# Low weight halves on GpSimd: one operation of 1024 columns, or four of 256

## The reference, cut to what matters

```
x = first_block(...)    # in-projection, short convolution + retention, out-projection, 16-expert FFN (top 32 tokens each)
x = second_block(...)   # in-projection, SSM + LRU mixer, projections, gated FFN with a convolution of 3 taps
return third_block(...) # an even layer (linear attention + sliding window), an odd layer (block attention), norm
```

```
def causal_dwconv(x, w, b):   # second block, K = 4 taps (20 tiles of 128 channels) and 3 taps (48 tiles)
    y[t] = b + sum(w[s] * x[t - s] for s in range(K))
```

## Time and profile before

| | |
|---|---|
| median of the runs | 2131.33 us |
| profiled execution | 2139.45 us |
| its span | 2137.7 us |
| PE busy | 1575.8 us (74%) |
| DVE busy | 758.0 us (35%) |
| POOL busy | 614.3 us (29%), 609.0 of it in L1354 |
| ACT busy | 579.0 us (27%) |
| DMA on the chain that ended last | 37% |

### The profile page before, as it was taken

How to read it: one execution, slowest core, us unless ns; L and a number is a source line. 1 busy time by engine, 2 the same in 40 slices (tenths; PEclk the granted TensorE clock), 3 DMA queues, 4 the chain that set the end, 5 groups by cost and what they waited for, 6 DMA issues and landing times.

```text
span 2137.7 us, 25344 instructions
## 1 busy us (share of the span) xinstructions
PE 1575.8 (74%) x10341; PEld 1066.2 (50%) x10341; DVE 758.0 (35%) x989; ACT 579.0 (27%) x973; POOL 614.3 (29%) x252
## 2 busy tenths in 40 slices
PE   4979786566566765666565689687789787889897
PEld 2758641111111211111111279676779777888797
DVE  3325420000000000000000189797839884176343
ACT  4324430000000000000000234645544344445453
POOL 1144300000000000000000058344648465655473
PEclk8989888877878687887878879899889897998898
DMA  9455559999999999999999825223325332433330
GB/s 395 141 200 229 236 236 428 428 429 428 429 429 428 429 429 428 430 428 428 430 428 429 381 99 186 90 80 118 119 79 197 118 124 112 166 140 113 115 119 20
DMA packets 48292, 570.06 MB, mean 267 GB/s; under 512 B 4576, under 2 KB 10720, under 8 KB 11744
## 3 DMA queue, kind: packets, MB, share of 16 engines
q1 hardware_dynamic: 40992, 556.81, 63.4%
q10 hardware_dynamic: 7232, 12.29, 2.1%
HBM read 564.89 MB, written 4.19 MB: 266 GB/s over the span
## 4 chain that ended last, share of the span: by engine, by line
DMA 37%; PE 29%; DVE 25%; ACT 3%; issue 2%; DVEq 1%; another core or an unknown queue 1%; ACTq 0%; POOL 0%; SPq 0%
PE bank L1373 29%; DMA ring<-in_w_down 12%; DMA ring<-in_w_up 12%; DMA ring<-in_w_gate 12%; DVE work L810 4%; DVE work L157 4%; DVE work L806 3%; DVE work L155 1%; ACT work L1689 1%; DMA ring<-in_dense 1%; DVE work L728 1%; DMA ring<-in_w_ada 1%; DVE rstd L1927 1%; DVE work L1931 1%; ACT weights_high_rounded L1689 1%
## 5 line engine op out<-in xcount | busy, mean ns | idle before, releaser
L1354 POOL TENSOR_TENSOR ring_rounded<-ring,weights_high_rounded 128x1024 fp32r<-128x1024 f32 x244 | 609.0, 2508 | 1475.1 <-ACT weights_high_rounded L1689 1474.3
L1373 PE MATMUL bank<-ring,work 128*32 128x512 f32 x3008 | 483.8, 776 | 309.7 <-DMA ring<-in_w_up 125.3
L1689 ACT ACTIVATE work<-bank 128x256 f32<-128x256 f32 (+3 forms) x312 | 137.5, 447 | 1188.5 <-PE bank L1373 833.4
L1373 PEld LDWEIGHTS bank<-ring,work 128*32 128x32 f32 x3008 | 93.1, 126 | 665.5 <-DMA ring<-in_w_up 207.6
L1689 ACT ACTIVATE weights_high_rounded<-ring 128x1024 fp32r<-128x1024 f32 x244 | 256.0, 1053 | 33.1 <-PE bank L1373 22.3
L1373 PE MATMUL bank<-h_high_rounded,weights_high_rounded 128*128 128x256 f32 x1296 | 208.6, 302 | 54.5 <-ACT weights_high_rounded L1689 35.9
L2140 DVE TENSOR_TENSOR work<-work,bank 128x512 f32<-128x512 f32 x16 | 16.5, 1030 | 592.3 <-PE bank L1373 592.3
L1373 PEld LDWEIGHTS bank<-h_high_rounded,weights_high_rounded 128*128 128x128 f32 x1296 | 178.7, 200 | 74.2 <-issue 39.3
L1373 PE MATMUL bank<-h_normed_rounded,weights_high_rounded 128*128 128x256 f32 x1296 | 187.1, 290 | 0.0
L1373 PE MATMUL bank<-h_high_rounded,ring_rounded 128*128 128x256 f32 x1296 | 182.8, 285 | 2.6 <-POOL ring_rounded L1354 2.5
L1373 PE MATMUL bank<-work_rounded,weights_high_rounded 128*128 128x256 f32 x1088 | 162.6, 301 | 29.1 <-ACT work_rounded L1689 20.2
(11 more groups left out here) (230 smaller groups left out, 1363.4 us busy)
## 6 DMA issues: line engine op xcount, KB each, us to landing
ring<-in_w_down SPq DMA_DIRECT2D x64, 2048.0 KB, 16.2
ring<-in_w_gate SPq DMA_DIRECT2D x63, 2048.0 KB, 16.2
ring<-in_w_up SPq DMA_DIRECT2D x61, 2048.0 KB, 16.4
ring<-in_dense SPq DMA_DIRECT2D x60, 2048.0 KB, 7.7
ring<-in_w_ada SPq DMA_DIRECT2D x12, 2048.0 KB, 20.4
work<-in_w_up SPq DMA_DIRECT2D x3, 1024.0 KB, 13.2
bias_diagonals<-work ACTq DMA_DIRECT2D x2, 1532.0 KB
ring<-in_dense SPq DMA_DIRECT2D x2, 1024.0 KB, 18.8
```

Source lines behind the costliest of these rows:

```text
L1354: nc.gpsimd.tensor_tensor(as_r(w), w, w_high[:, buffer, :], ALU.subtract).then_inc(s.w_low, 1)
L1373: return nc.tensor.matmul(o, lhsT, rhs, start=start, stop=stop)
L1689: return nc.scalar.activation(o, i, f, **kw)
```

## The change

The helper `low` issues four subtractions of 256 columns each, one behind the other, over the same unit and the same high buffer. Only the last one raises `w_low`. The wait for `w_high` stays ahead of the first. The four operations for the gather are as before.

```diff
             def low(block_no, sub, buffer):
                 w = unit_weights(block_no, sub)
-                nc.gpsimd.tensor_tensor(as_r(w), w, w_high[:, buffer, :], ALU.subtract).then_inc(s.w_low, 1)
+                for q in range(4):
+                    part = slice(q * SEQ, (q + 1) * SEQ)
+                    last = nc.gpsimd.tensor_tensor(as_r(w[:, part]), w[:, part], w_high[:, buffer, part], ALU.subtract)
+                last.then_inc(s.w_low, 1)
```

## The result

The changed kernel takes 2100.93 us (median of 4 runs, 2099.36 to 2106.62) against 2130.68 (4 runs) of the kernel before: ratio 0.9866, 95% interval 0.9846 to 0.9886, 30 us faster. The forecast was 65 us. The direction was right and the time lies inside the stated range (2035 to 2118 us), but the gain is less than half of the one forecast. The profiled execution took 2099.36 us, its span is 2097.6.

A forecast was written before the change was run, and what follows sets the result against it. No engine is full; DVE operations wait out long POOL operations on SBUF, and PE waits for DVE. Terms 14 + 9 + 6 + 25 + 16 - 5 = 65 us gained, giving 2066 us, range 2035 to 2118.

The forecast's parts named there:

- A quarter, 0.65 us: POOL's low halves: a 256-column operation comes every 0.65 us, so a free unit takes 2.65 us against PE's 2.79.
- Nothing fixed is paid again: Rival on POOL's low halves: quarter 0.60 us, unit 2.4 or 3.0, gain 85 us, total 2046 us; chance 0.12.
- A turn with a DVE operation, 0.80 us: Where POOL and DVE both have work, a quarter and a DVE operation alternate every 0.80 us (0.65 + 0.15).
- slack of 6.5 us: How far POOL may fall behind in a stretch of units before PE waits for it: 6.5 us.
- A: The 20-tile convolution from 1254 us: PE's 15.8 us wait on L157 goes, POOL falls behind; gain 14 us.
- B: The SSM heads: 14 POOL units in 85 us, shorter DVE waits beside each; gain 9 us.
- C: The mixing: PE's 10.2 us of waiting hangs on DVE, some ten POOL units; gain 6 us.
- E: Some eight short places where PE idles until DVE ends with POOL, softmax the largest at 4.6 us; gain 16 us.
- D: The FFN: PE ends its 48 units at 1742 instead of 1764 us, plus 3 in DVE's tail; gain 25 us.
- no turn between quarters: Rival: POOL keeps the way to SBUF over four quarters, DVE waits 2.65 instead of 2.41 us; 2143 us, chance 0.03.
- F: Places where PE already waits for POOL, and four units in a row at 78.66 us, grow longer; loss 5 us.
- The next wait is close: Rival: ACT's in-order work or PE's products hold the pace, so four gains give half; 2094 us, chance 0.15.

The follow-up runs named there:

- e8: The kernel before, unchanged, run and profiled a second time: 2131.65 us, profiled span 2130.8.
- e4: Changed kernel, with POOL waiting for its own last quarter's signal before each unit from the second set on: 2083.46 us, ratio 0.9794 to the kernel before.
- e2: Changed kernel with one operation of 1024 columns up to unit 144, four quarters only in the last 64 units (block 3): 2150.09 us.
- e6: Changed kernel with POOL's wait for its own last signal only ahead of each fourth unit in block 3: 2080.28 us.
- e1: Changed kernel with four quarters up to unit 144 of the second set, one operation of 1024 columns from there on: 2083.14 us.
- e7: Kernel before (whole units of 1024 columns) with POOL waiting for its own last signal ahead of every unit: 2140.53 us, ratio 1.0044.

## Why the prediction was right in direction and wrong in size

- **What bounds the kernel, and the mechanism: right.** DVE has little of the chain left, its waits shrank from 2.5 to 0.85 us, L157's wait went. One sentence is too wide: not every DVE operation with its inputs in SBUF waits. The reductions L1203 beside POOL and L1217 with POOL idle take the same 3.41 us for their two.
- **A quarter, 0.65 us: close, and too low at the point that matters.** The lower half of the distances between starts runs from 0.68 to 0.71 us; single quarters take 0.72 to 0.75. A unit takes 2.79 us from start to end at 2055.14, not 2.65:

```profile
2055.14 2.79 POOL L1356 TENSOR_TENSOR ring_rounded<-ring,weights_high_rounded 128x256 fp32r<-128x256 f32 x4 [11.25 <-ACT weights_high_rounded L1692]
```

  The forecast left 0.14 us of slack a unit; there is none. "Nothing fixed is paid again" is refuted. The estimate of 0.84 for a quarter and 0.79 for the spacing, which the prediction worked out from the figure of the Trainium skill ("GPSIMD Engine Reference", 3.1 Elementwise) for 2048 columns, is too high; the trace stands between it and mine, nearer to mine.
- **A turn with a DVE operation, 0.80 us: 0.87.** From unit 16 to 32 of the projection the changed kernel needs 51.4 us (1281.7 to 1333.1) where the kernel before needs 44.7 (16 x 2.79). That is 3.21 a unit, the pace that the forecast had (3.2), but its slack of 6.5 us doesn't show: the lag reaches PE with 6.7 us instead of 1.7. Over the next eight units the changed kernel makes up some 15 us (34.0 instead of 49.4), because the wait for L157 is gone.
- **A, gain 14: 8.3 measured** up to unit 40; the missing slack is 5.0 of the 5.7 between them.
- **B, gain 9: 0.8.** Mis-sized. The two or three operations of 0.28 us that were to wait are four of 0.3 to 0.4.
- **C, gain 6: 10.6, with the norms of E in it. D, gain 25: 28.2.** Right.
- **E, gain 16: the step that failed.** Some of it is in C's stage, but block 3, with the softmax taken as its largest place, gave 20.1 us back. What failed is a sentence: "between back-to-back operations DVE had its turn every time". It was true of every row of the first trace of before. That was in part luck: L1207 stood there behind four whole units without a gap and had its turn, and in the second profile of the same kernel (e8) it lost one. The rival built on its opposite, "no turn between quarters", was priced at one unit, 2.65 instead of 2.41 us, and given 0.03. The real thing is neither: turns are given in a dense exchange and can be lost in a long unbroken run, and an operation that has lost one waits until POOL stands still, up to 13 us. With the gap alone (e4) block 3 gains 2.5 us and the kernel lands at 2083, so even without the lost turns E was too large, by some 9 us: 16, less 2.5 and the 4.6 that C's stage has over its 6. Only 4.6 of its 16 us stood in a row.
- **F, loss 5:** PE's waits for POOL grew by 22.5 us (29.0 - 6.5), more than the "below 15" that the forecast allowed. With 40 waits for POOL between 1240 and 1780 us, each up to 1.9 us, one of its own signs of being wrong came in part: PE waits for POOL in the long runs of units.
- **The rival "The next wait is close"** gave 2094 us, nearer than the forecast. That is luck: it halved B, C, D and E alike, while C and D came in full, B not at all, and E with the opposite sign.
- **The base.** The forecast took its gain off the median, which is right; read off the two first traces the gain would be 40 us, 7 too many by e8.

The Trainium skill ("SBUF — State Buffer", Who interferes with whom) says that whoever issues first gets the shared port pair for the whole instruction, and the other is blocked. The trace agrees where the two take turns. It doesn't agree for the lost turns: L1207 is recorded as started at 1885.37, and sixteen quarters that started after it were done before it. The measurement decides here.

## What to carry to other kernels

Cutting a long GpSimd operation shortens the waits of VectorE beside it, and the gain follows the length of that wait; but the cut stops paying where the sum of the parts passes the pace of the engine that waits for them (here 2.79 us: four parts just over it, eight far over). Look for places where VectorE comes alone into a long back-to-back run of GpSimd operations, and break the run there (a wait of GpSimd for its own last signal is enough): such an operation can cost ten times its length or more. One profile that shows no lost turn doesn't rule them out. And judge the change stage by stage, by milestones that both kernels share: here +53 us in one part of the program and -20 in another made one mild ratio.

## What the runs showed of the hardware

- A two-input VectorE operation that meets a long unbroken run of GpSimd operations can wait through all of it: 16 columns took 11.43 us across 17 quarters, 1024 columns 13.14 us across 18, in both traces with quarters and no gap there (the changed kernel, e2). A gap of 0.14 us in GpSimd's stream ended the wait at once (e6).
- The same can happen beside operations of 1024 columns: 16 columns took 3.76 us across two of them (e8, e1), and 1.36 us in the first trace of the same kernel, with the same run before it.
- GpSimd's subtraction of 256 columns takes 0.72 to 0.75 us and starts every 0.68 to 0.71 when back to back; of 128 columns it starts every 0.41. In exchange with a two-input VectorE operation a quarter comes every 0.87 us.
- A wait of GpSimd for its own last signal leaves 0.14 us between two operations (e4: 1893.125 to 1893.268) that without it overlap by 0.04 in the record, and with whole units the run is 10 us longer (e7).
